# When a modulation column's block is read, and where the output gates' units stand around the layer norm

## The reference, cut to what matters

```python
for l in range(2):                                            # first block
    mx = split(silu(c) @ w_ada[l] + b_ada[l], 6)              # modulation, also mc from c_ctx
    hx, hc = modulate(rmsnorm(x)), modulate(rmsnorm(ctx))
    z = h @ w_in[l]                                           # q k v, o, gates, fourier, conv
    ym = layernorm_per_head(mlstm(q, k, v, gates)) * g * sigmoid(z[..., O_OFF:G_OFF])
    yv = silu(layernorm(dwconv31(a * sigmoid(gt)) + b_dw) * g_conv_ln + b_conv_ln)
    x = x + mx[2] * rmsnorm(concat(ym, fourier(u), yv) @ w_out[l])
    h = modulate(rmsnorm(x), mx[3], mx[4])
    x = x + mx[5] * rmsnorm(square(relu(h @ w_mlp1[l])) @ w_mlp2[l])
for l in range(2):                                            # second block: ada_w_2, retention,
    ...                                                       # sparse attention, gated linear attention
```

## Time and profile before

| | |
|---|---|
| median of 3 runs | 3344.05 us (3338.84 to 3344.07) |
| the profiled execution: own time, span of its instructions | 3338.16 us, 3336.4 us |
| PE busy | 3000.8 us (90%) |
| DVE, ACT, POOL busy | 1596.7, 1056.0, 1187.9 us |
| mean granted TensorE clock | 0.945 of full |
| MLP stage of layer 0, of layer 1 | about 545 to 1155 us, 1560 to 1995 us |
| output gates, layer norm and first half of `w_out`: layer 0, layer 1 | about 283 to 465 us, 1365 to 1506 us |

### The profile page before, as it was taken

The page is one execution under the profiler, slowest core; times in us unless marked ns, Lnnn a source line. Parts: engine busy times, 40 slices in busy tenths (PEclk is TensorE's granted clock), DMA queues, the critical chain, the costliest instruction groups (busy, mean ns, idle before and its releaser), DMA issues.

```text
span 3336.4 us, 41550 instructions
## 1 busy us (share of the span) xinstructions
PE 3000.8 (90%) x15908; PEld 2412.6 (72%) x15908; DVE 1596.7 (48%) x2851; ACT 1056.0 (32%) x1958; POOL 1187.9 (36%) x862
## 2 busy tenths in 40 slices
PE   7999788898899989968879899999989999999898
PEld 5788677777778867857657676777678767776786
DVE  4673535545555257344533214553482245544822
ACT  3224434121212231344222233233333322333332
POOL 1121142333333422214434452333255623332555
PEclk9999898999999989978989998999999989999999
DMA  5232011323233211103434321212112312221222
GB/s 202 90 138 76 13 55 53 102 101 109 94 114 107 66 57 63 58 23 101 145 106 154 119 89 67 74 64 64 61 60 73 93 64 70 64 70 57 62 75 67
DMA packets 78388, 276.98 MB, mean 83 GB/s; under 512 B 8544, under 2 KB 10848, under 8 KB 77936
## 3 DMA queue, kind: packets, MB, share of 16 engines
q1 hardware_dynamic: 75824, 268.91, 24.3%
q10 hardware_dynamic: 2368, 5.42, 0.4%
HBM read 272.19 MB, written 2.10 MB: 82 GB/s over the span
## 4 chain that ended last, share of the span: by engine, by line
PE 67%; DVE 15%; DMA 6%; ACT 5%; issue 4%; POOL 2%; SPq 0%; DVEq 0%; ACTq 0%; POOLq 0%
PE pb L1104 14%; PE pb L1105 14%; PE pb L1106 14%; DMA RG<-in_W_dram 6%; PE pb L1231 2%; DVE RLT L1861 2%; PE pb L1126 2%; PE pb L1128 2%; PE pb L1127 2%; PE pb L1143 1%; DVE AR L1822 1%; PE pb L1144 1%; PE pb L1145 1%; POOL RGR L2749 1%; PE pb L1189 1%
## 5 line engine op out<-in xcount | busy, mean ns | idle before, releaser
L2749 POOL TENSOR_TENSOR RGR<-RG,WHI 128x512 fp32r<-128x512 f32 x708 | 1002.5, 1426 | 1863.3 <-ACT WHI L2321 1862.3
L2321 ACT ACTIVATE WHI<-RG 128x512 fp32r<-128x512 f32 x708 | 432.5, 623 | 858.9 <-DMA RG<-in_W_dram 434.2
L1104 PE MATMUL pb<-HI,WHI 128*128 128x512 f32 (+1 forms) x880 | 374.8, 426 | 10.5 <-DVE LO L1750 4.9
L1106 PE MATMUL pb<-LO,WHI 128*128 128x512 f32 (+1 forms) x880 | 351.7, 400 | 0.0
L1105 PE MATMUL pb<-HI,RGR 128*128 128x512 f32 (+1 forms) x880 | 351.2, 399 | 0.0
L1104 PE MATMUL pb<-HR,WHI 128*128 128x512 f32 (+1 forms) x768 | 287.3, 374 | 68.0 <-POOL RGR L2749 61.6
L1104 PE MATMUL pb<-HIDR,WHI 128*128 128x512 f32 (+1 forms) x768 | 280.5, 365 | 42.4 <-POOL RGR L2749 17.1
L1106 PE MATMUL pb<-HR,WHI 128*128 128x512 f32 (+1 forms) x768 | 283.7, 369 | 0.0
L1105 PE MATMUL pb<-HR,RGR 128*128 128x512 f32 (+1 forms) x768 | 283.5, 369 | 0.0
L1105 PE MATMUL pb<-HIDR,RGR 128*128 128x512 f32 (+1 forms) x768 | 278.2, 362 | 0.0
L1106 PE MATMUL pb<-HIDR,WHI 128*128 128x512 f32 (+1 forms) x768 | 278.1, 362 | 0.0
(11 more groups left out here) (418 smaller groups left out, 5696.3 us busy)
## 6 DMA issues: line engine op xcount, KB each, us to landing
RG<-in_W_dram SPq DMA_DIRECT2D x504, 512.0 KB, 3.6
XCX<-in_xT_dram ACTq DMA_DIRECT2D x4, 512.0 KB, 11.8
out_dram<-XCX SPq DMA_DIRECT2D x8, 256.0 KB, 2.1
CS<-in_CST_dram ACTq DMA_DIRECT2D x1, 1027.0 KB, 4.8
XCC<-in_ctxT_dram SPq DMA_DIRECT2D x4, 256.0 KB, 13.7
AR<-in_VEC_dram ACTq DMA_DIRECT2D x1, 1024.0 KB, 6.3
CS<-in_CST_dram SPq DMA_DIRECT2D x1, 523.0 KB, 4.3
RG<-in_W_dram SPq DMA_DIRECT2D x2, 256.0 KB, 3.0
```

The source lines that it names most:

```text
L1104: e.matmul(out, hi[:, k, :], xh, start=k == order[0], stop=False)
L1106: i = e.matmul(out, hi[:, k, :], xl, start=False, stop=k == order[7])
L2321: e.activation(WHI[:, u % 2, h * n:h * n + n], RG[:, s % RING, h * n:h * n + n], ACT.Copy).then_inc(*up("weightsA", (u, h)))
L2749: e.tensor_tensor(RGR[:, s % RING, sl], RG[:, s % RING, sl], WHI[:, u % 2, sl].bitcast(F32), SUB).then_inc(*up("weightsG", (u, h)))
```

## The change

Two edits, and one line that lets the second name the right output rows.

1. `next_column` steps the oldest loaded column whenever one is loaded, where before it did so only when more than one was loaded (or none were left to ask for). A column is now read at the period after the one that asked for its slab, not at the second one after.
2. The four units of output gates are asked for one by one. In layer 0: unit 0, lnA of ctx, unit 1, lnB of ctx, unit 2, lnA of x, unit 3, lnB of x. In layer 1: unit 0, lnA of x, unit 1, lnB of x, then units 2 and 3 together. The two `weave` calls of 3.0 and 4.5 go, and the periods of the recurrence's steps are stretched ahead of the first mO (factor 1.22 for 1.05) and shortened behind it.
3. `tasks` adds an offset to the output row, so that a job of 128 columns writes its own rows.

```diff
     def next_column(self):
 
-        if self.loaded and (len(self.loaded) > 1 or not self.sums):
+        if self.loaded:
             self.step("column", self.loaded.pop(0))
...
-                new = {... "jj": j0 // 128, "j0": j0, ...}
+                new = {... "jj": j0 // 128 + more.get("j0", 0), "j0": j0, ...}
...
-    stages = o.begin(stages, [us * 1.05 / before] * before + [(us + 7.0) / (len(stages) - before)] * (len(stages) - before))
-    o.products([F(1536, 512, "og", "evacA", go)])
-    for t0, tn, _ in oregs:
+    stages = o.begin(stages, [us * 1.22 / before] * before + [us * 1.02 / (len(stages) - before)] * (len(stages) - before))
+    for i, (t0, tn, _) in enumerate(oregs):
+        o.products([F(1536 + 256 * i, 128, "og", "evacA", go, j0=2 * i)])
         o.run(o.piece("lnA", [], [o.bank()], ["evacV"], l=l, t0=t0, tn=tn, how="lnA"), [ALL8], 1.7)
-        o.weave(3.0)
+        o.products([F(1664 + 256 * i, 128, "og", "evacA", go, j0=2 * i + 1)])
         o.run(o.piece("lnB", [], [o.bank()], ["evacA"], l=l, t0=t0, tn=tn, how="lnB"), [ALL8], 1.7)
-    o.weave(4.5)
+    if l:
+        o.products([F(1792, 256, "og", "evacA", go, j0=2)])
```

More of the change, by code:

```diff
@@ L326, in tasks @@
                 c0 = cols[2 * t:2 * t + 2] if isinstance(cols, tuple) else cols + j0
-                new = {"kind": kind, "name": name, "l": l, "c0": c0, "w": w, "jj": j0 // 128, "j0": j0, "how": how, "by": by, "more": more}
+                new = {"kind": kind, "name": name, "l": l, "c0": c0, "w": w, "jj": j0 // 128 + more.get("j0", 0), "j0": j0, "how": how, "by": by, "more": more}
                 if kind == "T":
```

## The result

| | before | changed |
|---|---|---|
| median, range | 3341.45 us (3334.02 to 3344.07) | 3192.08 us (3190.71 to 3194.87) |
| ratio, 95% interval | | 0.9557 [0.9539, 0.9576] |
| profiled execution, span | 3338.16, 3336.4 | 3193.02, 3191.2 |
| PE busy, mean clock | 3000.8, 0.945 | 2956.1, 0.952 |

A forecast was written before the change was run, and what follows sets the result against it. PE was taken to bound the kernel, slowed by the ring in both MLP stages. 3338.16 - 141 (part 1) - 20 (part 2) = 3177 us, stated as 3178; range 3150 to 3225, the forecast's own 3155 to 3200.

The forecast's parts named there:

- the ring: Both MLP stages, relu2 units: column read, transfer, split and evacuation wait in a circle, 12.20 and 9.93 us per unit; -141 us.
- part 2: Stages ahead of both MLPs: layer norm placed among the output gates, -17 us in layer 1, about -3 in layer 0, -20 together.
- The ceiling of 147.4: Units 4 to 55 of both MLP stages: distance to PE's own pace, 74.9 us in layer 0 and 72.5 in layer 1.
- The 3 us per layer: MLP stages: taken off the gain in each layer for transfers that land late.
- idle at about half: Layer 1 ahead of its MLP, 1436 to 1530 us, shifted: PE's idle time of 23.5 us was to fall to about half.
- The other two waits of mO: Layer 0 ahead of its MLP: of PE's three waits of mO for gating, 12.4 us together, two keep their place.
- The two half-steps moved to the end: Layer 0's `w_out` stage: two more half-steps of the recurrence there end behind the products, charged 3 us.
- Part 1: MLP stages of both layers: gain from reading columns a unit earlier, -141 us, bounds 0 and -147.
- Rival (a): Layer 1's MLP: the ring stays there, half of 72.5 us is not gained, 3214 us; chance 0.12.
- (b): Stages ahead of both MLPs: layer norm moved to the wrong place, +14 instead of -20, 3212 us; chance 0.09.
- (c): MLP stages: the column edit does nothing, slabs are late because of their own slot, 3318 us; chance 0.04.
- (d): MLP stages: slower, DVE reaches a column read before its slab has landed and holds evacuations, up to 3548 us; chance 0.02.

The follow-up runs named there:

- e2: The changed kernel with the old condition in `next_column`, so the edit of output gates and layer norm alone; 3337.3 us, ratio 0.9981.
- e1: The kernel before with the column edit alone; 3200.2 us, ratio 0.9568.
- e5: The kernel before; in the MLP stages ACT converts a unit's first half behind the last evacuation of the unit two before it; 3207.7 us, ratio 0.9588.
- g2: The kernel before with two more DVE passes over each column slab of layer 1; 3427.1 us, ratio 1.0257.
- e3: The changed kernel with layer 0's layer norm at its old place and with its old periods; 3186.6 us, ratio 0.9527.
- g1: The changed kernel with two more DVE passes over each column slab of layer 1; 3252.2 us, ratio 0.9727.
- g4: The changed kernel, measured again; 3195.2 us, ratio 0.9560.
- f1: The changed kernel with layer 0's layer norm at its old place but with the new periods; 3187.0 us, ratio 0.9533.
- f3: The changed kernel with layer 0's layer norms starting a unit earlier and periods factors 1.18 and 0.90; 3194.4 us, ratio 0.9552.

## Why the prediction was right, and where not

The range held the result because the ring is 141 of the forecast's 161 us and was well priced. The rest, part 2, was forecast at -20 and was -6.3 (3.3 to 9.4) alone, in e2, and -0.3 in the profiles of before and changed.

*The ring and its price: right.* The turn through DVE's read, SP, the transfer, the split and the evacuation was the cause, shown by cutting it at two different links (e1, e5). Its signs held: cycles of 134.67 and 89.32 us for 135 and 89 forecast, clock 1.00, SP's waits halved, ACT's waits for slabs 84.8 us for 434.2. The ceiling of 147.4 was reached to within 0.5: 75.1 and 71.8 us between units 4 and 55 in the profile (e2 against the changed kernel: 71.6 and 72.2). The 3 us per layer that I took off for transfers landing late were not needed. So -141 was 6 too small by the profiles; the timed runs of e1 (-144, from -139 to -149) can't tell the two apart. Idle time alone would have returned 44.1 us in two cycles, idle time and clock 62.8; they returned 29.0 and 33.6, together 62.6. PE's busy time in them fell by 9.2 and 9.3 (143.89 to 134.67, 98.59 to 89.32, at clock 0.96 and 0.93 before and 1.00 after), which is the clock, as the Trainium skill ("TensorE: Matmul & The Clock Gate", HAM oscillation) has it for loops that wait for a transfer.

*Part 2, layer 1: right in kind, -9 for -17.* The waits for ACT's square (9.0) and behind mA (5.8) are gone. The changed kernel waits instead

```profile
PE pb L1386 <- DVE AR L1966: 5.7, 2, 4.1
PE pb L1160 <- POOL MXL L2765: 4.8, 1, 4.8
PE pb L1160 <- DVE AR L1844: 4.2, 2, 3.3
PE pb L1408 <- DVE AR L2034: 3.9, 1, 3.9
```

for a split (4.8, was 1.2) and for the last gating (3.9, new); the stretch has 55.1 us idle for 63.0. I had booked 4 us for such returns; the rows of waits give 7.5. Of the 6 us of clock that I added, PE's busy time shows 1.2 (422.6 for 423.9). The sign "idle at about half" failed: the same 94 us of layer 1, shifted by 72, have 20.3 us idle for 23.5. Over all profiles the stretch "to L1" is 490.0 with the old place (before, e1, e5, g2) and 477.9 with the new (nine profiles), 12 less: 8 of it idle time, the rest the clock's share, in which single profiles differ as much.

*Part 2, layer 0: wrong sign, +9 for -3.* "To L0" is 553.2 on average with the old place (before, e1, e3, e5, g2), 559.8 with the new (changed, e2, g1, g4); these 7 us are idle time. The wait at the first product with `w_out` was called well: 8.4, 3.7 + 4 forecast. The first mO's 4.8 went as well: in its place stand 0.5 and, at the mA behind it, 1.3. What failed is this. The other two waits of mO were to keep their size, 3.0 and 4.5; they are 4.3 and 8.8, the last because its gating has nothing over it. The chain that ended last in the changed kernel, at the end of that stage, shows it:

```profile
461.29 2.77 DVE AR L2026 x3
464.05 0.60 DVE AR L1844
464.65 1.04 DVE AR L2034 x4
465.83 1.09 PE pb L1408 x4
```

The two half-steps moved to the end were priced at 3; the last wait alone grew by 4.3. Two waits I had not booked: evacuations of `w_out` pieces on DVE, 8.8 for 4.1, and the sigmoids of output gates behind the layer norm on ACT, 4.3, both in the first list under f1 to f3. Against them PE's waits in mA to mD fell by some 8. And the 5 us of clock did not come: 0.85 for 0.87 from 283 us on, and over those same profiles PE's busy time up to the MLP stage is 479.2 us for 479.7.

*The sum.* Against the profiled execution the forecast was 3177. Part 1 came out 6 better, layer 1 8 worse, layer 0 12 worse, and 2 us came outside these four stretches: 3177 - 6 + 8 + 12 + 2 = 3193, the profiled time. The 3178 that I said was meant for a median and took off only 1 of the 6 us between the two; by my own sum it should have been 3183, and the measured median is 3192.1. Rival (a) did not occur (pitch 5.58 in all of layer 1); (b) occurred in layer 0 alone, while layer 1 made up for it; (c) fell with the gain of e1; (d) fell, since no row of DVE's waits names a column's slab.

## What to carry to other kernels

When several waits of a few microseconds repeat once per unit, follow them round: a ring sets the pace by its turn, and it could be cut here at either of two links (an earlier read, or an evacuation put ahead of a convert that waits), for nearly the whole distance to the bound engine's pace and the clock beside it. That a turn over two units counts half for each fits all runs, but none isolates it. In e5 late transfers did no harm, since no evacuation stood in order behind them. Where the path is a chain of short dependent steps on several engines, as in the recurrence here, a named wait that is removed can return under another name, or ahead of the stage that one looks at, as f3's did: price what the moved work uncovers at its new place, and compare PE's idle time over the whole way there. Test by stage, since +7 and -8 us of idle time look like one small gain. Don't book a return of the clock for a few microseconds of idle time: of 5 and 6 us forecast, none and 1.2 came.

## What the runs showed of the hardware

The clock's dips are not a property of the program alone: in e1 PE's instructions of the stretch "to L1" are those of before in the same order, and took 429.41 us of busy time for 423.85. So single profiles of one program differ by up to 7 us in a stretch of 490, and an edit of that size needs many profiles or medians, or PE's idle time, which agreed within 2.1 us in the four profiles of that program (62.7 to 64.8).

A DVE pass over a column slab (128x1024, two inputs) took between 1.21 and 2.31 us, and what decides it is which of the two began first, it or POOL's low-part subtraction. In the changed kernel, among the passes that stand singly in the timeline from 600 to 1740 us, 75 began with no subtraction running and took 1.21 to 1.22 us; 53 began while one ran and took 1.44 to 2.31. The subtraction is the same from its side: 60 that began while a pass ran took 2.14 to 2.36 us, the other 132 between 1.26 and 1.86, most of them 1.29 (its mean over the whole kernel is 1436 ns). So the one that starts second takes up to 1.1 us more, and the first is not slowed. The rows of g1 above show both: the subtraction at 1616.30, behind a pass begun at 1616.29, takes 2.33, and of the two passes together (3.43) the second carries the delay. The Trainium skill names the contention in "GPSIMD Engine Reference", section Specifications: the two engines share SBUF interfaces and contend where DVE has two SBUF inputs. The rows of g1 agree. The price of a pass in a place where POOL works was then nearer 1.6 us than 1.24 (mean 1.59 in g2, 1.73 in g1).
